# Sample attention: one 32-column group of the array for each pair of heads

## The reference

```
k_all = concatenate([cache_k, new k])          # 2048 + 8 positions per sequence
for window, dil in ((128, 1), (512, 4), (2048, 16)):
    idx = 2048 + t - dil * arange(window // dil + 1)
    s = (q . k_all[idx]) * 64 ** -0.5;  p, lse = softmax(s);  o = p . v_all[idx]
out = sum over branches of softmax(lse) * o
```

## Time and profile before

| | us |
|---|---|
| runs | 2010.55, 2011.19, 2023.85; median 2011.19 |
| span of the profiled execution | 2013.2 |
| TensorE busy | 1742.1 (87%) |
| TensorE weight loads | 1337.4 (66%) |
| DVE, ACT, POOL busy | 759.6, 465.9, 469.1 |
| granted TensorE clock, mean of the span | 0.925 |

### The profile page before, as it was taken

One profiled execution on the slowest core, in us unless ns is written; L12 is line 12 of the kernel. 1 busy time (PEld: TensorE's weight loads), 2 busy tenths in 40 slices (PEclk: granted clock), 3 DMA queues, 4 the chain that ended last, 5 costly groups with the idle time before them and its releaser, 6 DMA issues. The chain is left out here.

```text
span 2013.2 us, 22061 instructions
## 1 busy us (share of the span) xinstructions
PE 1742.1 (87%) x8144; PEld 1337.4 (66%) x8144; DVE 759.6 (38%) x1384; ACT 465.9 (23%) x710; POOL 469.1 (23%) x218
## 2 busy tenths in 40 slices
PE   6599999959896754888889679999999999999990
PEld 1488888847775643444348558888888888888880
DVE  4921122036554744221112343333333333333368
ACT  0422222225553210211112231211111111111111
POOL 0233333220001510000003252222222222222243
PEclk9799999979998655999989889999999999999995
DMA  7544343341102217777451311111111111111114
GB/s 260 189 161 144 139 168 121 116 136 48 58 0 71 80 33 198 205 209 191 123 176 43 111 53 42 42 42 42 42 42 42 52 51 51 50 46 42 42 31 142
DMA packets 135863, 192.86 MB, mean 96 GB/s; under 512 B 9339, under 2 KB 84139, under 8 KB 135604
## 3 DMA queue, kind: packets, MB, share of 16 engines
q1 hardware_dynamic: 123542, 169.16, 27.0%
q10 hardware_dynamic: 12272, 23.07, 3.1%
HBM read 163.20 MB, written 29.00 MB: 95 GB/s over the span
## 5 line engine op out<-in xcount | busy, mean ns | idle before, releaser
L1960 DVE TENSOR_TENSOR res<-res,ps 128x512 f32<-128x512 f32 x256 | 175.7, 688 | 156.2 <-PE ps L2028 155.8
L1800 POOL TENSOR_TENSOR mlp_w_lo<-mlp_w_raw,mlp_w_hi 128x2048 fp32r<-128x2048 f32 x32 | 147.5, 4612 | 336.0 <-ACT mlp_w_hi L1796 333.1
L1993 PE MATMUL ps<-mix_hi,mlp_w_hi 128*128 128x512 f32 x512 | 205.1, 401 | 6.8 <-POOL mlp_w_lo L1800 4.8
L2028 PE MATMUL ps<-mlp_w_hi,mlp_h_hi 128*128 128x512 f32 x512 | 201.1, 393 | 6.2 <-PE ps L1999 5.4
L1993 PE MATMUL ps<-mix_lo,mlp_w_hi 128*128 128x512 f32 x512 | 202.4, 395 | 0.0
L1993 PE MATMUL ps<-mix_hi,mlp_w_lo 128*128 128x512 f32 x512 | 201.8, 394 | 0.0
L2028 PE MATMUL ps<-mlp_w_hi,mlp_h_lo 128*128 128x512 f32 x512 | 199.4, 389 | 0.0
L2028 PE MATMUL ps<-mlp_w_lo,mlp_h_hi 128*128 128x512 f32 x512 | 199.3, 389 | 0.0
L1936 DVE TENSOR_TENSOR mlp_h_lo<-mlp_pos,mlp_h_hi 128x512 fp32r<-128x512 f32 x64 | 65.1, 1018 | 326.6 <-ACT mlp_h_hi L1882 324.4
L557 POOL TENSOR_TENSOR inp_a_lo<-inp_room,inp_a_hi 128x2048 fp32r<-128x2048 f32 x24 | 110.6, 4609 | 216.2 <-ACT inp_a_hi L600 216.2
L579 PE MATMUL ps<-inp_whi,z_hi 128*128 128x512 f32 x384 | 151.5, 395 | 10.6 <-DVE inp_wlo L529 7.8
(11 more groups left out here) (337 smaller groups left out, 2938.4 us busy)
## 6 DMA issues: line engine op xcount, KB each, us to landing
mlp_w_raw<-in_w_ff SPq DMA_DIRECT2D x32, 1024.0 KB
inp_room<-in_w_ada SPq DMA_DIRECT2D x16, 1024.0 KB
proj<-inp_row ACTq DMA_DIRECT2D x54, 256.0 KB, 2.4
K<-in_cache_k SPq DMA_DIRECT2D x48, 256.0 KB, 6.4
cache_V<-in_cache_v SPq DMA_DIRECT2D x48, 256.0 KB
mod_w<-in_w_ada SPq DMA_DIRECT2D x4, 2048.0 KB, 15.6
inp_room<-in_w_ada_f SPq DMA_DIRECT2D x8, 1024.0 KB
x<-in_w_in ACTq DMA_DIRECT2D x16, 512.0 KB, 6.6
```

The source lines that it names most:

```text
L1800: pool.tensor_tensor(lo, raw[:], hi.bitcast(F32), ALU.subtract).then_inc(ready, 1)
L1960: dve.tensor_tensor(dst, dst, ps[:, 5 + o % 3, :], ALU.add).then_inc(added, 1)
L1993: mm = pe.matmul(ps[:, u, :], w[:, k, j * P:(j + 1) * P], z[:, k, rows], start=(k == 0 and a == 0), stop=(k == KT - 1 and a == 2))
L2028: mm = pe.matmul(out, h, w, start=(a == 0), stop=(a == len(parts) - 1))
```

## The change

Each pair of heads gets 32 columns of its own: `QCOLS` = 32 columns hold sequence 0's two heads (16 columns) and sequence 1's (16), zero in the half that belongs to the other sequence. A score product now writes rows 32 c to 32 c + 31; the accumulator adds up over the two sequences b, three steps apart, and not over c. A value product takes the 32 probability columns of one pair of heads and streams only that pair's 128 value columns, so 44 products replace 11 for a sequence; the results of the two sequences stand beside each other in 256 columns of which each row keeps its own. Row order becomes c, b, head in the pair, token. The query blocks are half as large and written in 16 pieces, not 8; scaling, row transposes (2 for 4) and the copies out (2 for 4 on each of ACT and DVE, twice as wide) follow. Loads, their order and the order of the steps stay.

```diff
--- before.py
+++ after.py
@@ -53,6 +53,7 @@
 OLD = 1536
 KTILES = 10
 NKEYS = KTILES * P + DS
+QCOLS = 4 * DS
 GF = 256
 NG = FF // GF
 
@@ -1298,10 +1299,13 @@
                 steps.done(dve.tensor_tensor(k_masked[:, h], dup.unsqueeze(1).broadcast_to([NS, 4, P]), din[:, h], ALU.mult))
 
             dve.wait_ge(att_turned, 1)
+            blocks = q_blocks[:].rearrange("p (i b) c n -> p i b c n", b=2)
             for h in range(H):
                 rows = slice(HD * (h % 2), HD * (h % 2 + 1))
-                src = ps[rows, 0, (h // 2) * NS:(h // 2 + 1) * NS].rearrange("p (b t) -> p b t", b=DB)
-                steps.done(dve.tensor_scalar(q_blocks[rows, :, h // 2, h * DS:(h + 1) * DS], src, SCALE, None, ALU.mult))
+                src = ps[rows, 0, (h // 2) * NS:(h // 2 + 1) * NS].rearrange("p (i b t) -> p i b t", b=2, t=DS)
+                for b in range(2):
+                    first = QCOLS // 2 * b + DS * (h % 2)
+                    steps.done(dve.tensor_scalar(blocks[rows, :, b, h // 2, first:first + DS], src[:, :, b], SCALE, None, ALU.mult))
             steps.done(dve.tensor_copy(kT_new[:], ps[:, 0, 4 * NS:8 * NS].rearrange("p (c n) -> p c n", n=NS)))
             dve.wait_ge(ret_turned, 1)
             steps.done(dve.tensor_copy(flat(qT), ps[:, 1, 0:RH * NS]))
@@ -1387,12 +1391,12 @@
         bias = st.sb("bias", [P, NKEYS])
         V = [st.sb(f"V{b}", [P, KTILES, AW]) for b in range(2)]
         v_new = [st.sb(f"v_new{b}", [DS, AW]) for b in range(2)]
-        q_now = st.sb("q_now", [P, 2, 4, NS])
+        q_now = st.sb("q_now", [P, 2, 4, QCOLS])
         k_now = st.sb("k_now", [P, 4, 2 * DS])
         kT = [st.sb(f"kT{s}", [P, 4, CH]) for s in range(2)]
         prob = st.sb("prob", [P, NKEYS])
         probT = st.sb("probT", [P, KTILES + 1, P])
-        rows = st.sb("rows", [P, AW])
+        rows = st.sb("rows", [P, 2 * P])
         top, neg, total, inv, waited = (st.sb(n, [P, 1]) for n in ("top", "neg", "total", "inv", "waited"))
         mix_f = st.sb("mix_f", [P, 4, NS])
         v_in = [st.sem(f"v_in{b}") for b in range(2)]
@@ -1449,8 +1453,8 @@
                 if n == 0:
                     pe.wait_ge(q_staged, 2 * i + 2)
                 for c in range(4):
-                    mm = pe.matmul(ps[NS * b:NS * (b + 1), 4 + n % 3, 0:w], q_now[:, b, c, :], kT[n % 2][:, c, 0:w],
-                                   start=(c == 0), stop=(c == 3))
+                    mm = pe.matmul(ps[QCOLS * c:QCOLS * (c + 1), 4 + n % 3, 0:w], q_now[:, b, c, :], kT[n % 2][:, c, 0:w],
+                                   start=(b == 0), stop=(b == 1))
                 mm.then_inc(scored, 1)
                 if n % 3 == 2:
                     pe.wait_ge(scored, 6 * i + n + 1)
@@ -1469,21 +1473,25 @@
                 pe.wait_ge(pT_dve, 2 * j + 2)
 
             def values(j, b):
-                cols = slice(NS * b, NS * (b + 1))
                 if b == 0:
-                    pe.wait_ge(out_dve, 4 * j + 4)
+                    pe.wait_ge(out_dve, 2 * j + 2)
                 pe.wait_ge(v_in[b], 16 * 8 * j + 16 * 8)
-                for t in range(KTILES):
-                    pe.matmul(ps[cols, 7, :], probT[:, t, cols], V[b][:, t, :], start=(t == 0), stop=False)
-                mm = pe.matmul(ps[cols, 7, :], probT[0:DS, KTILES, cols], v_new[b][:], start=False, stop=True)
+                for t in range(KTILES + 1):
+                    keys = slice(0, P if t < KTILES else DS)
+                    for c in range(4):
+                        cols = slice(QCOLS * c, QCOLS * (c + 1))
+                        heads = slice(c * P, (c + 1) * P)
+                        mm = pe.matmul(ps[cols, 7, b * P:(b + 1) * P], probT[keys, t, cols],
+                                       V[b][:, t, heads] if t < KTILES else v_new[b][:, heads],
+                                       start=(t == 0), stop=(t == KTILES))
                 mm.then_inc(pv_made, 1)
                 pe.wait_ge(pv_made, 2 * j + b + 1)
                 pe.sem_inc(v_free, 1)
 
             def turn_rows(j):
                 pe.wait_ge(rows_done, j + 1)
-                for c in range(4):
-                    mm = pe.transpose(ps[:, 7, c * P:(c + 1) * P], rows[:, c * P:(c + 1) * P], ident[:])
+                for b in range(2):
+                    mm = pe.transpose(ps[:, 7, b * P:(b + 1) * P], rows[:, b * P:(b + 1) * P], ident[:])
                 mm.then_inc(rows_turned, 1)
 
             def pair(i, first=False):
@@ -1516,12 +1524,11 @@
             values(j, 1)
             turn_rows(j)
 
-        def head_rows(j, h):
-
-            part = slice(HD * (h % 2), HD * (h % 2 + 1))
-            src = ps[part, 7, (h // 2) * P:(h // 2 + 1) * P].rearrange("p (b h t) -> p b h t", b=2, t=DS)[:, :, h, :]
-            dst = mix_f[part, h // 2, ds(j * 2 * DS, 2 * DS)].rearrange("p (b t) -> p b t", b=2)
-            return dst, src
+        def head_rows(j, b, h):
+
+            part = slice(HD * h, HD * (h + 1))
+            src = ps[part, 7, b * P:(b + 1) * P].rearrange("p (c b h t) -> p c b h t", b=2, h=2, t=DS)[:, :, b, h, :]
+            return mix_f[part, :, ds(j * 2 * DS + b * DS, DS)], src
 
         @block.scalar
         def _(act):
@@ -1537,8 +1544,8 @@
             def take_rows(j):
 
                 act.wait_ge(rows_turned, j + 1)
-                for h in range(0, H, 2):
-                    dst, src = head_rows(j, h)
+                for b in range(2):
+                    dst, src = head_rows(j, b, 0)
                     act.copy(dst, src).then_inc(out_act, 1)
 
             def pair(i, first=False):
@@ -1562,13 +1569,13 @@
             exponent(PAIRS - 1)
             take_probs(PAIRS - 1)
             take_rows(PAIRS - 1)
-            act.wait_ge(out_act, 4 * PAIRS)
-            act.wait_ge(out_dve, 4 * PAIRS + 4)
+            act.wait_ge(out_act, 2 * PAIRS)
+            act.wait_ge(out_dve, 2 * PAIRS + 2)
             act.copy(mix_s[:, 0:4, 0:NS], mix_f[:]).then_inc(hi_done, 1)
 
         @block.vector
         def _(dve):
-            dve.sem_inc(out_dve, 4)
+            dve.sem_inc(out_dve, 2)
             dve.wait_ge(tables, 16)
 
             def softmax_top(j):
@@ -1589,12 +1596,12 @@
             def scale_rows(j):
                 dve.wait_ge(pv_made, 2 * j + 2)
                 dve.wait_ge(inv_done, j + 1)
-                dve.tensor_scalar(rows[:], ps[:, 7, :], inv[:], None, ALU.mult).then_inc(rows_done, 1)
+                dve.tensor_scalar(rows[:], ps[:, 7, 0:2 * P], inv[:], None, ALU.mult).then_inc(rows_done, 1)
 
             def take_rows(j):
-                dve.wait_ge(out_act, 4 * j + 4)
-                for h in range(1, H, 2):
-                    dst, src = head_rows(j, h)
+                dve.wait_ge(out_act, 2 * j + 2)
+                for b in range(2):
+                    dst, src = head_rows(j, b, 1)
                     dve.tensor_copy(dst, src).then_inc(out_dve, 1)
 
             def pair(i, first=False):
@@ -2142,7 +2149,7 @@
             stage_prompt_attention(nc, io, ps, ident, mix_hi, mix_lo)
             stage_prompt_retention(nc, io, ps, ident, mix_hi, mix_lo)
             with ExitStack() as cc:
-                q_blocks, kT_new = held(cc, "q_blocks", [P, DB, 4, NS]), held(cc, "kT_new", [P, 4, NS])
+                q_blocks, kT_new = held(cc, "q_blocks", [P, DB, 4, QCOLS]), held(cc, "kT_new", [P, 4, NS])
                 K = [held(cc, f"K{b}", [P, KTILES, AW]) for b in range(2)]
                 k_in = [cc.enter_context(nc.semaphore(f"k_in{b}")) for b in range(2)]
                 stage_sample_heads(nc, io, ps, ident, mix_s, q_blocks, kT_new, K, k_in)
```

## The result

The changed kernel takes 1961.81 us (median of 4 runs, 1958.53 to 1969.51), the kernel before 2015.11 beside it: a ratio of 0.974 [0.969, 0.979]. The forecast was 1970 (1950 to 1988), worked out from 2011.19.

A forecast was written before the change was run, and what follows sets the result against it. The prediction took TensorE to bound the kernel at 54.6 us a pair, transfers hidden behind it. Its terms summed to -40.9 us, from a 2013.2 span to 1972.3, or 1970 as a median; range 1950 to 1988.

The forecast's parts named there:

- query blocks: Stage before sample attention: 16 writes of 32 columns for 8 of 64, in DVE's chain, +1.6 us.
- to the start of pair 1: Stage start up to 833.35: K's landing sets it, TensorE waits instead of computing, 0 us.
- pair 1 to its third chunk: 833.35 to 864.8: two score chunks, one short chunk and one value product shorter, +3.4 for half clock; -6.2 us.
- two periods: Loop becomes transfer-bound, second sequence's K transposes queued before the third chunk: 45.5 us each for 54.6, -18.2 us.
- third chunk of pair 3 to the end: Stage end: three value products, score chunks and output transposes shorter, clock +1; -18.1 us.
- The value product: Per sequence, 88 records at 63 ns plus 0.5: 6.0 us for 10.14, saves 4.1; ends 2.9 and 10.1 us.
- The score chunk: 512-column chunk on TensorE: 1.3 us for 3.48, midway between two and four overlapping groups, saves 2.2.
- the bounds: All four groups overlap at full clock, score chunks 2.6 us lower in all: -52 us, 1959; with values at 27 ns, 1947.
- The clock: Pair 1 after its K wait: half clock adds 1.7 for transposes, 1.3 for probability transposes, 0.4 for a chunk; +3.4 us.
- that rival: TensorE's clock stays at its lower level through most of the stage: 1982, or 1996 with two groups overlapping; chance 0.12.
- no overlap: 32-column groups do not overlap: value products 9.6 us per sequence, chunks unchanged, 2013 us; chance 0.06.
- exposed loads: Score and value products: each change of column group exposes a 137 ns weight load, 61 us, 2074; chance 0.05.

The follow-up runs named there:

- the kernel run again: The changed kernel, unaltered, measured a second time: 1958.56 us, 0.972 of the kernel before.
- e10: Changed kernel with every K and V load after the first pair cut to 4 of its 10 tiles, on all partitions: 1919.96 us, 0.953 of the kernel before.
- e1: Changed kernel with a sequence's 44 value products ordered group by group instead of going round the four groups: 1988.38 us, 0.988 of the kernel before.
- e9: Changed kernel with value products streaming 64 of each head pair's 128 value columns: 1959.09 us, 0.974 of the kernel before.
- e7: Changed kernel with pair 1's second K load issued only once its first K has landed: 1952.40 us, 0.970 of the kernel before.
- e2: Kernel before with the changed value products alone, scores as they were: 1981.94 us, 0.981 of the kernel before.

## Why the prediction was right, and where its terms were off

| step | forecast us | measured us |
|---|---|---|
| query blocks | +1.6 | +0.1 |
| to the start of pair 1 | 0 | +3.6 |
| pair 1 to its third chunk | -6.2 | -12.7 |
| two periods | -18.2 | -17.9 |
| third chunk of pair 3 to the end | -18.1 | -27.6 |
| sum | -40.9 | -54.5 |

**The mechanism held.** The two periods came out as written: first K issue to last K landed 41.2 and 40.3 us (855.89 to 897.11, 902.11 to 942.39), half-clock transposes 3.6, the short chunk and the issue. Single periods agree that closely in part by luck: the kernel run again has 49.8 and 41.9 us, nearly the same sum. They are bound by transfers (e10), through the wait that was named: the transposes of the second sequence's K ahead of the third chunk. Of the signs, the waits for K of 10.10 and 10.92 us and the gap of 5.0 us in the transfers came as written; the records 62 ns apart and the stage 42 us shorter did not. In pair 1 and in the last pair, where TensorE is on the path, its shorter products count in full: e1's four value products are 7.9 us longer each, and those two parts 31.2 us.

**The value product was mis-sized**: "88 x 63 ns + 0.5 = 6.0 us", and it takes 3.14. The four of them on the path (one in pair 1, three at the end) gave 10.3 us more than priced: 10.14 to 3.14 in pair 1; at the end 10.14, 11.4 and 9.8 to 3.2, 4.7 (the one at half clock) and 2.8. The 63 ns of the earlier trace rows were read as a floor on issue. e9's 15.4 ns refutes that for records of different groups; why line 240's transposes start 63 ns apart stays open. Their weights fill all 128 columns (9*128 in the earlier trace rows), so no two of them are in different groups, and this difference from the 32-column products was not weighed. What was called the lower end, four groups at full overlap, is what happened.

By the page "TensorEngine Tiling (Array Packing)", "Instruction Overhead" (the Trainium skill), about 60 cycles each, some 25 ns as an estimate, the sum would have been 1958, nearer the result. Yet the runs don't show such an overhead paid record after record either: e9 has 15.4 ns.

**The score chunk** takes 0.88 us, not 1.3, for the same reason. The four chunks on these two parts gave 0.8 us more than priced, and not 1.6, because the steps behind two of them wait for copies (0.17 and 0.41 us, the "up to 0.4" that the prediction left out). In the bounds the chunks' 2.6 is 2.2 by the prediction's own terms, which moves 1959 by 0.4.

**The clock** was charged +3.4 in pair 1 for transposes, probability transposes and a chunk. Only the 16 transposes ran at the lower level (3.67 us for 1.96): at 842.12, after another 1.36 us of waiting, the probability transposes took 1.40 us, and the chunk 1.06. And only 0.6 of their 1.7 us reached the path. From the transposes to the probability transposes it takes 5.04 us (837.08 to 842.12) for 4.44 before, when TensorE waited longer for the copies in between (timeline of the kernel before):

```profile
837.79 1.42 PE L1464 MATMUL ps<-ident,cache_prob 128*128 128x128 f32 x11 [2.48 <-ACT cache_kT L1553]
```

So 0.6 of the 3.4. The +1 at the end is part of the 4.7 us of the second value product above, and no cost beside it. In pairs 2 and 3 the probability transposes did take 2.58 us, inside the transfer-bound periods, where it cost nothing.

**The query blocks** did cost 0.6 us in their own row, 16 in 2.54 us for 8 in 1.99. VectorE's timeline of the changed kernel:

```profile
767.52 2.54 DVE L1308 TENSOR_SCALAR q_blocks<-ps 64x32 f32<-64x32 f32 x16
...
790.77 2.48 DVE L1327 SCALAR_TENSOR_TENSOR smp_state<-smp_state,ps 128x512 f32<-128x512 f32 x4 [14.91 <-PE ps L1373]
```

But VectorE then waits 14.91 us for TensorE and goes on 0.1 us later than before (790.67 there). The blocks were priced as part of a chain without looking for the wait that ends last in it.

**The start of pair 1** was called 0 because "K's landing sets it". It does, and the change moved that landing: TensorE finishes pair 0's keys sooner, so SP issues the second K load at 823.49 instead of 833.07, while the first (816.65) is still under way. SP's timeline, changed kernel:

```profile
816.65 3.75 SPq L1211 DMA_DIRECT2D K<-in_cache_k  x6
820.45 0.59 SPq L1212 DMA_DIRECT2D K<-in_cache_k  x1
823.49 4.07 SPq L1211 DMA_DIRECT2D K<-in_cache_k  x6
```

With both under way the first K is waited for until 837.08, for 833.35. e7, which holds the second load, took the 3 us back there, and the next period lost them.

**The rivals.** The clock did fall to 0.75 and 0.77 of full speed in the periods, but it came back to full speed between waits (16 transposes in 1.94 us at 905.51), so only a part of that rival is true. Groups overlap fully, so there is no case of no overlap. Nor of exposed loads: a load of line 1484 lasts 110 ns (median), and records begin 28.8 ns apart.

The rule cited against the change, of "TensorE: Matmul & The Clock Gate", "The mechanism" (the Trainium skill), that loads overlap running products only in another row group, does not describe this kernel: in the stretch 849.90 to 850.06 eight loads run beside eight products that all use 128 rows.

By these terms (values 10.3, chunks 0.8, clock 2.8 and 1.0, query blocks 1.5, less 3.6 for the start and 0.3 for the periods) about 1.1 of the 13.6 us between the two sums is assigned to no step. Why four loads of equal size take from 38 to 49 us in these runs (37.7 in the kernel run again, 48.8 in e2) was not settled; a load of the next pair that is issued early may be part of it.

## What to carry to other kernels

Small fp32 products whose weights fill 32 columns each should go to the four column groups in turn, innermost: the order of issue alone was worth 26 us here, all of it where TensorE was on the path. Before pricing such a change, ask what the shorter work will be bound by, and price that to the microsecond; here four loads, the half-clock transposes behind them and one short chunk set both periods, and the other products cost nothing in them. And look behind each transfer for the one that an earlier release will put beside it.

## What the runs showed of the hardware

- fp32 products in four column groups begin four within 30 ns, then none for 70, 28.8 ns a record on average; with 64 columns streamed instead of 128 it is 15.4 ns. In one group at a time (e1) twenty records take what eighty take in four.
- Loads into 64 of 128 partitions with half the bytes took 35.9 us for four at 148 GB/s, where loads on all partitions ran at 228 to 283 over whole periods: they saved little.
- With a second K load issued 6.8 us behind it, a K load landed 20.4 us after its issue (816.65 to 837.08); with the second held (e7), 16.8 us (809.21 to 826.01).
